# Building the expert gates of a PEER layer with 256 indirect accumulating transfers into DRAM instead of one-hot products

## The reference, cut to what matters

```python
s_top, i_top = lax.top_k(s, PEER_TOPK)                 # 16 best of 128 keys, 8 heads x 2 halves
cand = s_top[:, :, 0, :, None] + s_top[:, :, 1, None, :]
sc, ci = lax.top_k(cand, PEER_TOPK)                    # 16 best of 256 pairs, per token and head
experts = e_a * PEER_N_KEYS + e_b                      # e_a, e_b: the keys of the pair
gw = jax.nn.softmax(sc, axis=-1)
act = jax.nn.gelu(jnp.einsum('td,tkd->tk', xb, u_tab[eb]), approximate=False)
out = jnp.einsum('tk,tkd->td', gb * act, v_tab[eb])    # 8 x 16 = 128 experts per token
```

## Time and profile before

| | before |
|---|---|
| median of 3 runs | 1806.13 us (1805.28 to 1807.16) |
| span of the profiled execution | 1795.7 us |
| between that span and the median | 10.4 us, ahead of the first instruction and behind the last |
| PE busy | 1744.2 us, 97% |
| DVE / ACT / POOL busy | 1251.2 / 942.1 / 492.9 us |
| granted clock of PE | 0.994 of full |
| HBM read / written | 328.84 / 17.83 MB |

### The profile page before, as it was taken

The page is one execution under the profiler, slowest core; times in us unless marked ns, Lnnn a source line. Parts: engine busy times, 40 slices in busy tenths (PEclk is TensorE's granted clock), DMA queues, the critical chain, the costliest instruction groups (busy, mean ns, idle before and its releaser), DMA issues.

```text
span 1795.7 us, 33010 instructions
## 1 busy us (share of the span) xinstructions
PE 1744.2 (97%) x11190; PEld 1547.2 (86%) x11190; DVE 1251.2 (70%) x2359; ACT 942.1 (52%) x1389; POOL 492.9 (27%) x225
## 2 busy tenths in 40 slices
PE   9999989999999999999999999999999999999997
PEld 6799878897878999999999988888888787669996
DVE  4567587876424499067777578888888896667777
ACT  5466577544555544567777643333333575334444
POOL 4246744401568588800000000000000100013332
PEclk9999999999999999999999999999999999999999
DMA  6654443577344478755565687677767783355553
GB/s 216 200 188 141 166 152 118 190 248 266 121 164 150 135 222 228 228 179 172 174 173 173 195 263 239 235 235 236 237 239 236 272 276 122 113 176 187 183 183 113
DMA packets 122839, 347.63 MB, mean 194 GB/s; under 512 B 13904, under 2 KB 46800, under 8 KB 122512
## 3 DMA queue, kind: packets, MB, share of 16 engines
q1 hardware_dynamic: 121248, 339.52, 58.1%
q0 software_dynamic: 1520, 7.21, 1.1%
HBM read 328.84 MB, written 17.83 MB: 193 GB/s over the span
## 4 chain that ended last, share of the span: by engine, by line
PE 84%; DVE 6%; ACT 4%; issue 2%; POOL 2%; DMA 1%; POOLq 0%; DVEq 0%; ACTq 0%
PE banks L934 83%; POOL weight_rest L851 2%; ACT arena L1676 2%; DMA weight_ring<-in_stream 1%; ACT weight_high L1676 1%; PE banks L945 1%; DVE weight_rest L2307 1%; ACT span_exponentials L1676 0%; DVE arena L3110 0%; DVE arena L2991 0%; DVE arena L2348 0%; ACT scratch L1676 0%; ACT L1676 0%; DVE arena L2347 0%; DVE arena L2345 0%
## 5 line engine op out<-in xcount | busy, mean ns | idle before, releaser
L1676 ACT ACTIVATE weight_high<-weight_ring 128x1024 fp32r<-128x1024 f32 x448 | 473.0, 1057 | 453.4 <-PE banks L934 350.4
L851 POOL TENSOR_TENSOR weight_rest<-weight_ring,weight_high 128x1024 fp32r<-128x1024 f32 x165 | 414.4, 2521 | 264.5 <-ACT weight_high L1676 155.0
L2307 DVE TENSOR_TENSOR weight_rest<-weight_ring,weight_high 128x1024 fp32r<-128x1024 f32 x283 | 346.1, 1224 | 156.3 <-ACT weight_high L1676 153.4
L934 PE MATMUL banks<-a_high,weight_high 128*128 128x256 f32 x1216 | 304.0, 288 | 0.2 <-ACT weight_high L1676 0.2
L934 PE MATMUL banks<-a_rest,weight_high 128*128 128x256 f32 x1216 | 297.8, 283 | 0.0
L934 PEld LDWEIGHTS banks<-a_high,weight_high 128*128 128x128 f32 x1216 | 232.6, 191 | 1.5 <-issue 1.1
L934 PEld LDWEIGHTS banks<-a_rest,weight_high 128*128 128x128 f32 x1216 | 232.9, 192 | 0.3 <-issue 0.2
L934 PE MATMUL banks<-weight_high,gated_high 128*128 128x512 f32 x512 | 201.4, 393 | 0.0
L934 PE MATMUL banks<-weight_high,gated_rest 128*128 128x512 f32 x512 | 200.2, 391 | 0.0
L934 PE MATMUL banks<-a_high,weight_rest 128*128 128x256 f32 x1216 | 170.9, 283 | 2.4 <-POOL weight_rest L851 2.4
L934 PE MATMUL banks<-x_high,weight_high 128*128 128x256 f32 x672 | 167.5, 287 | 4.7 <-DVE x_rest L3079 3.7
(11 more groups left out here) (360 smaller groups left out, 3101.5 us busy)
## 6 DMA issues: line engine op xcount, KB each, us to landing
weight_ring<-in_stream SPq DMA_DIRECT2D x512, 512.0 KB, 3.5
arena<-in_stream SPq DMA_DIRECT2D x66, 512.0 KB, 3.3
unit_spill<-small SPq DMA_DIRECT2D x128, 128.0 KB, 3.6
scratch<-unit_spill SPq DMA_DIRECT2D x128, 128.0 KB, 3.2
residual<-in_x SPq DMA_DIRECT2D x2, 512.0 KB, 4.1
arena<-in_mem POOLq DMA_DIRECT2D x2, 512.0 KB, 5.3
arena<-in_ctx POOLq DMA_DIRECT2D x2, 512.0 KB, 4.8
arena<-in_keys POOLq DMA_DIRECT2D x1, 1024.0 KB, 5.2
```

What stands on the lines that cost most here:

```text
L851: nc.gpsimd.tensor_tensor(w_lo[:, e % 2, :], raw(e)[0], w_hi[:, e % 2, :], ALU.subtract).then_inc(S["rest_ready"], 1)
L934: return nc.tensor.matmul(out, lhsT, rhs, start=start, stop=stop, skip_group_check=True)
L1676: return nc.scalar.activation(out, in_, f, **kw)
L2307: tt(w_lo[:, e % 2, :], raw(e)[0], w_hi[:, e % 2, :], ALU.subtract).then_inc(S[ready], 1)
```

## The change

The map of gates is made in DRAM. Its 16 MB (`gate_map`) are cleared by 32 transfers of 512 KB, which SP issues behind 32 of the fetches of the cross attention and the queries (`CLEARED`), from a buffer that POOL sets to zero. DVE works out the address of each gate, (e_a x 128 + e_b) x 256 + token, in float32, and casts it (`gates`). POOL then issues 256 indirect transfers, one for each of two halves of the tokens and 128 choices: each adds 128 gates, one per token, to 128 addresses. Within a half, the 16 transfers of a head wait for all those of the head before, as two heads may have chosen one expert. Six heads of the first half go alone (`SOLO`), then the heads of the second half, with the last two of the first half in between. SP loads the map back row by row (`load_gates`), the first time when all 256 transfers have landed.

The units stay in SBUF, in `WT`. POOL makes the rests of only the first 22 units; DVE makes those of the other 106 and fits 39 of them among the instructions of the second half's choice (`among_keys`, `among_pairs`). Operations of `best_pairs(1)` over 2048 elements are cut in two. The turned numbers, the one-hot matrices, their products and the copies into the map go. `cH` moves to units 14 and 22, and the two exponentials to units 22 and 62.

```diff
-UD = U0 + 52
-U_EARLY, U_EXP, U_GATED = 52, 48, 64
+U_KEYS, U_POOL, U_PAIRS, U_TAIL = 14, 22, 62, 122
+SOLO = 6
+UD = U0 + U_POOL
+CLEARED = [g for g, (kind, sec, i) in enumerate(RING_TILES)
+           if kind == SPLIT and sec in ("cross_q", "ctx", "cross_out", "peer_q")][4:36]
...
+            def load_gates(a):
+                if a == 0:
+                    for t in range(TT):
+                        sp.wait_ge(scattered[t], 16 * PSLOT)
                 if a >= 4:
                     sp.wait_ge(S["p_ready"], a - 3)
-                sp.dma_start(UNITS_IN[:, a % 4, :], spill[a]).then_inc(h_in[a % 4], 16)
+                sp.dma_start(GATES_IN[:, a % 4, :], gate_tiles[a]).then_inc(gates_in[a % 4], 16)
...
+                if g in CLEARED:
+                    sp.wait_ge(S["clear_made"], 1)
+                    sp.dma_start(gate_parts[CLEARED.index(g)], CLEAR).then_inc(gates_cleared, 16)
+                if sec == "values" and i == 0:
+                    for a in range(4):
+                        load_gates(a)
+                if sec == "values" and i >= 4:
+                    load_gates(i)
...
+            def scatter(t, h):
+                if h == 0:
+                    pool.wait_ge(S["idx_ready"], t + 1)
+                else:
+                    pool.wait_ge(scattered[t], 16 * PTOP * h)
+                for k in range(PTOP):
+                    n = t * P + h * PTOP + k
+                    pool.indirect_dma_start(
+                        gate_map, bass.IndirectOffsetOnAxis(ap=EXPERT_U[:, n:n + 1], axis=0), GATE[:, n:n + 1], None,
+                        compute_op=ALU.add).then_inc(scattered[t], 16)
+
+            pool.wait_ge(gates_cleared, 16 * 32)
+            for h in range(SOLO):
+                scatter(0, h)
+            for h in range(PH):
+                scatter(1, h)
+                if SOLO + h < PH:
+                    scatter(0, SOLO + h)
...
+            units(2, U_KEYS)
+            context_state(0)
+            units(U_KEYS, U_POOL)
+            context_state(1)
+            units(U_POOL, P - 2)
...
-                func(UNITS[:, slot, :], arrived(act, job, turn)[:, 0:T], ACT.Gelu)
+                func(WT[:, r, :], b[:, 0:T], ACT.Gelu)
...
             def gates(t):
                 g3 = EAB[:, t, 2, :].rearrange("p (h k) -> p h k", h=PH)
+                a, b = EAB[:, t, 0, :], EAB[:, t, 1, :]
+                step(stt(b, a, float(P), b, ALU.mult, ALU.add))
+                step(stt(b, b, float(T), NUMBER[:, t:t + 1].to_broadcast([P, P]), ALU.mult, ALU.add))
+                cp(EXPERT_U[:, tsl(t)], b)
                 dve.wait_ge(S["gate_exp"], t + 1)
...
+            def among_keys(n, g):
+                if g in ((), (5, 7, 9, 11, 13, 15), (7, 15), (3, 7, 11, 15))[n]:
+                    unit_rest()
+                if n == 1 and g == 7:
+                    gates(0)
+
+            def among_pairs(n, g):
+                if g in ((3, 7), (1, 2, 4, 5, 7), (3, 7), (2, 5, 7))[n]:
+                    unit_rest()
...
-                    for v in range(4):
-                        slot = bass.ds(i * 16 + (4 * u + v), 1)
-                        ins = ts(ROWHOT[:, u % 2, v, :], C("iota"), slots[:, 0, slot], slots[:, 2, slot],
-                                 ALU.is_equal, ALU.mult)
```

More of the change, by code:

```diff
@@ L999, in split_block, with split_channels @@
                     split_tile(e + j, None, 0, high, rest, *rest_count(e + j))
-            def split_channels(e, job, hi, lo_, turn, n, rest_ready, rest_count, part=0, parts=1, half=None):
-                b = claim(job, turn) if part == 0 else bank(job)
+            def split_channels(e, job, hi, lo_, turn, n, rest_ready, rest_count, part=0, parts=1, half=None, more=None):
+                if more is not None:
+                    b = claim(job, 0 if turn is None else turn, more)
+                else:
+                    b = claim(job, turn) if part == 0 else bank(job)
                 at = KC * part
@@ L1370, in _, with unit, units, context_state @@
                     filled(ins, ("ce", d, t))
-            def units(a, job, turn):
+            def unit(a, turn=None):
                 e = U0 + a
                 ready, count = rest_count(e)
[L1376 to L1386, removed]
+                if turn is None:
+                    split_channels(e, ("unit", a % 4), a3_hi, a3_lo, None, 4, ready, count, more=a // 4)
+                else:
+                    split_channels(e, ("unit", a % 4), a3_hi, a3_lo, turn, 4, ready, turn * 4 + count, more=a // 4)
+            def units(a, b):
+                with pe.Fori(0, (b - a) // 4) as i:
+                    for j in range(4):
+                        unit(a + j, i)
+            def context_state(d):
+                pe.wait_ge(S["ctx_kd"], 1)
                 b = claim(("cH", d))
@@ L1392, in _ @@
                 filled(ins, ("cH", d))
[L1394 to L1402, removed]
-                    for v in range(4):
[L1404 to L1409, removed]
+            for a in range(2):
+                unit(a)
+            units(2, U_KEYS)
[3 more added lines that the diff above has]
+            units(U_POOL, P - 2)
+            for a in range(P - 2, P):
+                unit(a)
             def split_sums(e, name, hi, lo_, turn, n, rest_ready, rest_count, last=False):
@@ L2042, in _, with unit_out, units_out @@
-            for t in range(TT):
+            def unit_out(a, turn=None):
+                job = ("unit", a % 4)
+                b = arrived(act, job, 0 if turn is None else turn, a // 4)
+                r = unit_row(a)
+                r = r if turn is None else turn * 4 + r
+                free(func(WT[:, r, :], b[:, 0:T], ACT.Gelu), job)
+            def units_out(a, b):
+                with act.Fori(0, (b - a) // 4) as i:
+                    for j in range(4):
+                        unit_out(a + j, i)
+                        split_high(U0 + a + j + 2, i, 4)
@@ L2065, in dense @@
[L2065 to L2078, removed]
-                for u in range(4):
-                    unit_and_gates(i, u)
-                    if u == 2:
-                        columns(i + 1)
@@ L2083, in _ @@
[L2083 to L2089 removed]
+            for a in range(2):
+                unit_out(a)
+                split_high(U0 + a + 2)
+            units_out(2, U_KEYS)
@@ L2091, in _ @@
+            evacuate(("cH", 0), h0[:, 0], src=quarters)
+            units_out(U_KEYS, U_POOL)
+            evacuate(("cH", 1), h0[:, 1], src=quarters)
+            gate_exp(0)
+            units_out(U_POOL, U_WRAP)
+            units_out(U_WRAP, U_PAIRS)
+            gate_exp(1)
+            units_out(U_PAIRS, U_TAIL)
+            for a in range(U_TAIL, P):
+                unit_out(a)
+                split_high(U0 + a + 2)
             with act.Fori(0, P // 4 - 1) as i:
@@ L2788, in _ @@
-            with dve.Fori(0, U_LATE // 4) as i:
-                for j in range(4):
-                    split_rest(UD + U_GATED + j, "lo_ready", i, 4)
-            for u in range(4):
-                freed(dve, ("w", u), T // 16 - 1)
+            while unit_at[0] < U_PAIRS + 4:
+                unit_rest()
+            with dve.Fori(0, (P - 2 - U_PAIRS - 4) // 4) as i:
+                for j in range(U_PAIRS + 4, U_PAIRS + 8):
+                    split_rest(U0 + j, "lo_ready", i, 4)
+            for a in range(P - 2, P):
+                split_rest(U0 + a, "lo_ready")
@@ L2806, in gate_row, with gate_rows @@
                 tt(gated_lo[:, s, :], GATED[:, s, :], gated_hi[:, s, :], ALU.subtract).then_inc(S["p_ready"], 1)
+            def gate_rows(a, b):
+                with dve.Fori(0, (b - a) // 4) as i:
+                    for j in range(4):
+                        split_rest(V0 + a + j - 2, "lo_ready", i, 4)
+                        gate_row(a + j, i)
             gate_row(0)
             gate_row(1)
-            for a in range(4):
-                split_rest(V0 + a, "lo_ready")
-                gate_row(a + 2)
@@ L2813, in _ @@
-            with dve.Fori(0, P // 4 - 2) as i:
-                for a in range(4, 8):
-                    split_rest(V0 + a, "lo_ready", i, 4)
-                    gate_row(a + 2, i)
-            for a in range(P - 4, P):
+            gate_rows(2, U_WRAP)
+            gate_rows(U_WRAP, U_TAIL)
+            for a in range(U_TAIL - 2, P):
                 split_rest(V0 + a, "lo_ready")
```

198 lines of the change are left out of this document (84 added, 114 removed).

## The result

The changed kernel takes 2007.47 us (median of 4 runs, 2006.44 to 2012.01) against 1805.7 us for the kernel before: a ratio of 1.113, 95% interval 1.111 to 1.115. It is 202 us slower, where 54 us less were forecast.

A forecast was written before the change was run, and what follows sets the result against it. PE was taken to bound the kernel: 57.4 us less from removed products and stalls, plus 1 for ports and 2 for clears, gives -54.4 us, with scatters hidden. Forecast 1752 us, range 1744 to 1798.

The forecast's parts named there:

- What bounds the kernel: PE, busy in 97% of the span; units, gates and values lie on its chain, so removed products give their time back.
- what is removed: One-hot products 56.3 us, turning 0.7 and stalls 2.0, less 1.6 of stalls that stay: stage ends 57.4 us sooner.
- The clears: Zeroing 16 MB during earlier fetches could make tiles late: 2 us taken, from 0 to 8.
- The rests: DVE's 39 rests among the second half's searches are hidden by PE's 2.88 us per unit; shared ports cost 1 us, 0 to 5.
- The scatters: POOL's 256 indirect transfers, started at 690, end at 981, 5 us before the values need them at 986: cost nothing.
- the term c: POOL's time for one indirect transfer, taken as 0.97 us, bounded by 0.57 below and 2.4 above.
- the prediction's own formula: With no idle time POOL's transfers end at 690 + 256c + 11L; past 986, each us is a us of PE.
- L: Time from a head's last issued transfer to its landing: between 3.2 and 4.8 us, taken as 3.5.
- Rival (B): Transfers so slow that the stall eats the gain, from c = 1.22; at c = 1.4, 1853 us; chance 0.08.
- rival (C): Port lock: each of DVE's 106 rests holds POOL for 1.22 us, 129 us in all, 1871 us; chance 0.05.
- The row at 1056: Profile row where POOL issues a transfer in 0.57 us beside DVE's two-SBUF-operand products, neither holding the other.
- Rival (D): Small packets take 102 to 205 us of 16 transfer engines, making weights up to 65 us late, 1817 us; chance 0.04.

The follow-up runs named there:

- no_scatter: Changed kernel without the 256 indirect transfers, rows of the map loaded from the weights in DRAM, product with gates left out: 1748.57 us, 0.969 of the kernel before.
- one_sbuf: Changed kernel with DVE's 106 rests of the units subtracting PSUM numbers, so only one operand is in SBUF: 1957.26 us.
- fixed_no_add: Changed kernel with each indirect transfer replaced by an ordinary one of POOL writing 128 single numbers to fixed places, without addition: 1751.41 us.
- no_add: Changed kernel with the 256 indirect transfers writing instead of adding: 1986.08 us.

## Why the prediction was wrong

**What bounds the kernel, and what is removed: right.** The sum without transfers, -54.4 us, was measured as -55.2 (`no_scatter`). That it fits to 0.8 us is in part luck: from PE's first unit to its first product of the values it was 431.6 us before (616.75 to 1048.30) and is 378.0 now (620.10 to 998.05), 53.6 less where 57.4 - 1 = 56.4 were forecast, and the 2 us for the clears weren't needed. Most of the 2.8 is a term that the sum lacks: the last eight products of two units in a row start 2.88 us apart, but 21 times, at every fourth unit, 3.07, with no wait in the profile; what makes it isn't known. The clears cost nothing that can be seen: the stretch from 447.9 to 588.5 us, with them, took 140.6 us, and the same chain of work before took 140.7, from 441.9 to 582.6; the transfer engines' share in it is 0.78, less than the 0.9 allowed for. The rests fit among the searches: the waits of the changed kernel show none on PE between 690 and 996 us.

**The scatters: this step failed, in the term c, "I take c = 0.97".** It was made from the ordinary transfer's 0.57 plus 0.4 for reading addresses. That is right to 0.01 for an indirect transfer that writes, 0.96 (the runs don't show how much of the 0.43 over the ordinary one is reading addresses). What was missing is the addition, 0.59 more, and a gap of 0.30 between two: 1.85 us per transfer. By the prediction's own formula, 690 + 256 x 1.85 + 11 x 3 = 1197 against 986, 211 us late, 1963 us. `one_sbuf`, which has just this and no hold, took 1957. L was put at 3.5; it is 3.0 where the transfers run alone and 3.0 to 5.5 beside the units, and the waits between heads, 21 us, were less than allowed for. Two of the signs that the prediction gave for being wrong, c over 1.0 and longer transfers where DVE makes rests, are thus both there.

**Rival (B) is what happened, and rival (C) came on top.** (B) put the turning point at c = 1.22; it was given 0.08 since "the ordinary transfer's 0.57 would have to more than double". It did: 0.57 to 1.85. (C) had 1.22 us per rest, 129 in all; the measured hold is 53 us (50 in time), as only transfers that start within a rest are held, and only for what is left of it. The row at 1056 spoke against (C) and misled: it is an ordinary transfer, which reads no addresses, and `fixed_no_add` shows that such transfers aren't held. The rule weighed there, in the Trainium skill's "SBUF — State Buffer", "SBUF: two separate sides", on two SBUF inputs against GpSimd work that reads SBUF, is borne out for the indirect transfer by 1.55 against up to 2.6 us, but in one direction only: the rest at 908.70, which starts within a transfer, keeps its 1.23 us. The 102 cycles per small read in the Trainium skill's "GPSIMD Engine Reference", "Performance pitfalls for Q7 kernels", are for code of one's own on GpSimd; the transfer doesn't pay them: 128 rows take 1.55 us and not 11.

**Rival (D) didn't happen.** While the transfers run alone, from 996 to 1246 us, the transfer engines' share is 0.22, 0.22 x 250 x 16 / 130 = 6.8 us of one engine for each of the 130 transfers there, near the lower end of the 6.4 to 12.8 that it had. No weights were late.

**A mistake without effect.** I put 10.4 us between the span and the median. In four runs of the changed kernel there are 1.8 (2006.96 against 2005.2). So the profiled execution of before was itself some 8 us shorter than the median, if the 1.8 hold there too. Since the sum was a difference, the forecast didn't depend on it.

The range was wrong for one reason more: with c bounded only by 0.57 and 2.4, and the turning point at 1.22, more than half of the interval lay on the slow side, and my chances gave it 0.16.

## What to carry to other kernels

An indirect transfer of 4 bytes a row that adds costs POOL 1.41 us for 64 rows and 1.55 for 128, so by estimate some 1.3 before the first row, and 0.30 of gap on top: count transfers, not rows. 256 of them are 474 us on POOL, for some 55 us that the rest of the change gives on PE; use them only up to the time that something else hides. If one unmeasured price multiplied by 256 decides a change, the range must reach to both of its bounds.

## What the runs showed that was not expected

The indirect transfers that write instead of adding made the kernel slow in another way. Their last one started at 1074, 169 us sooner than in the changed kernel, yet the time fell by only 21 us, for PE was slow beside them, and the transfer engines' share was low (`no_add`, span, busy by engine, PEclk, share, GB/s; then PE in order of time):

```profile
996.00:1076.00 80.00, 10.16 (x31) 7.82 (x29) 2.45 (x2) 1.33 (x2) 58.31 (x60) 0.50 0.06 14
```

```profile
938.10 0.37 PE L954 MATMUL banks<-a_rest,weight_high 128*128 128x256 f32 x1 [2.43 <-issue]
940.90 0.37 PE L954 MATMUL banks<-a_high,weight_high 128*128 128x256 f32 x1 [2.43 <-issue]
943.70 0.37 PE L954 MATMUL banks<-a_rest,weight_high 128*128 128x256 f32 x1 [2.43 <-issue]
```

The products start 2.80 us apart, and the profile shows nothing that PE waits for in between. ACT and DVE wait for up to 66 us for an event that the profile can't place. It isn't the weights, as the expectation of `fixed_no_add` had it: SP fetches a tile only when a rest has released its slot, for which it waits up to 66.8 us, and the tile that it fetches at 904.16 has its 128 rows under way by 906.9; the share is low because little is asked for. Once the transfers are over, PE works at its usual pace (from 1088.8 on). Ordinary transfers writing 4 bytes each to fixed places (`fixed_no_add`) don't do this, nor do indirect ones that add. Why stays open; it wasn't tried further.

The hole in the changed kernel also let PE's granted clock fall to about half, 1.2 of 2.4 GHz: 0.52 from 996 to 1246 us, when PE was idle. It cost little: the clock is 0.61 from 1250 to 1256 and 0.99 over the values after it, 1250 to 1600. The values last 359.1 us from their first product to their last, against 354.5 before and in `no_scatter`.
